# A one-core decoder step in which 14 of the weight loads are sent as transfers of 63, 63 and 2 partitions

## The reference, cut to what matters

```python
def retrieve(hb):
    q = (hb @ wq).reshape(chunk, PEER_HEADS, 2, PEER_HALF)      # 1024 -> 2048 columns
    s = jnp.einsum('nhcd,hckd->nhck', q, sk)                    # 8 heads x 2 x 128 keys
    sv, si = lax.top_k(s, 16)
    ...                                                        # the best 16 of 16x16 sums
    expert = i1 * N_KEYS + i2                                   # one of 16384 experts
    g = jax.nn.softmax(cs, axis=-1)
    act = gelu(einsum('nd,nhkd->nhk', hb, u_tab[expert]))
    return einsum('nhk,nhkd->nd', g * act, v_tab[expert])
```

## Time and profile before

| | us |
|---|---|
| median of 3 runs (lowest, highest) | 3008.63 (3007.17, 3009.83) |
| profiled execution, its own time | 3011.34 |
| its span, from the first to the last instruction | 3009.4 |
| TensorE busy in the span | 2609.7 |
| VectorE busy | 2108.1 |
| bytes moved | 1214.93 MB, mean 404 GB/s |

### The profile page before, as it was taken

The page is one execution under the profiler, slowest core; times in us unless marked ns, Lnnn a source line. Parts: engine busy times, 40 slices in busy tenths (PEclk is TensorE's granted clock), DMA queues, the critical chain, the costliest instruction groups (busy, mean ns, idle before and its releaser), DMA issues.

```text
span 3009.4 us, 27506 instructions
## 1 busy us (share of the span) xinstructions
PE 2609.7 (87%) x7369; PEld 1282.4 (43%) x7369; DVE 2108.1 (70%) x5150; ACT 1285.6 (43%) x3706; POOL 1206.2 (40%) x1104
## 2 busy tenths in 40 slices
PE   8989999999988888888899889887899977777777
PEld 6675565555544443333444434333444422222222
DVE  3546766788766667777667677778676766777666
ACT  2123444655444434444443444345443444444444
POOL 2103443444444444444443444444343434334442
PEclk9999999999999999999999999999999999999999
DMA  9979999999999999999999999999999999999997
GB/s 346 334 280 366 382 421 410 417 395 411 422 421 421 421 421 413 421 422 394 422 421 419 381 421 416 421 422 412 421 416 419 410 421 406 420 422 410 420 414 319
DMA packets 175000, 1214.93 MB, mean 404 GB/s; under 512 B 19730, under 2 KB 20766, under 8 KB 33269
## 3 DMA queue, kind: packets, MB, share of 16 engines
q0 software_dynamic: 155904, 1124.11, 91.0%
q1 hardware_dynamic: 18941, 89.07, 7.6%
HBM read 1208.47 MB, written 38.37 MB: 414 GB/s over the span
## 4 chain that ended last, share of the span: by engine, by line
DMA 45%; PE 37%; DVE 8%; ACT 6%; issue 3%; POOL 1%; another core or an unknown queue 0%; DVEq 0%; SPq 0%; ACTq 0%; POOLq 0%
DMA RING<-in_peer_uv,idx 44%; PE PSUM L1291 22%; PE PSUM L974 10%; DVE RING L1998 5%; ACT diag L1489 2%; PE PSUM L985 1%; ACT L1480 1%; ACT gate L1485 1%; PE PSUM L956 1%; ACT act_h L1480 1%; PE PSUM L1279 1%; POOL RING L922 1%; ACT L1468 1%; DMA RING<-in_peer_uv,pidx 1%; PE PSUM L995 0%
## 5 line engine op out<-in xcount | busy, mean ns | idle before, releaser
L1291 PE MATMUL PSUM<-RING,diag 128*128 128x512 f32 (+1 forms) x4096 | 1977.2, 619 | 364.4 <-ACT diag L1489 358.0
L922 POOL DMA_INDIRECT RING<-in_peer_uv,idx x1024 | 1155.8, 1129 | 1593.5 <-PE PSUM L1291 1481.2
L1998 DVE CUSTOM_DVE_ANT_0 RING<-RING,H 128x1024 f32<-128x1024 f32 x1032 | 1263.5, 1225 | 650.2 <-DMA RING<-in_peer_uv,idx 636.1
L1291 PEld LDWEIGHTS PSUM<-RING,diag 128*128 128x128 f32 (+1 forms) x4096 | 737.9, 192 | 1446.0 <-ACT diag L1489 820.3
L1480 ACT ACTIVATE act_h<-dots 128x1 f32<-128x1 f32 x1040 | 208.2, 200 | 1112.5 <-DVE dots L1998 1110.8
L1489 ACT ACTIVATE diag<-ident,gate 128x128 f32<-128x128 f32 x1008 | 404.8, 402 | 33.1 <-PE PSUM L1291 0.3
L974 PE MATMUL PSUM<-HT,WCH 128*128 128x256 f32 (+2 forms) x1408 | 335.0, 385 | 1.5 <-ACT HT L1344 1.3
L1485 ACT ACTIVATE gate<-act_h,ex 128x1 f32<-128x1 f32 x1008 | 296.8, 294 | 32.7
L974 PEld LDWEIGHTS PSUM<-HT,WCH 128*128 128x128 f32 x1408 | 265.3, 192 | 90.9 <-issue 59.2
L1480 ACT ACT_TABLE_LOAD x91 | 116.8, 1283 | 6.9 <-DVE dots L1998 5.3
L1344 ACT ACTIVATE YT<-PSUM 128x256 f32<-128x256 f32 (+4 forms) x70 | 27.4, 391 | 191.4 <-PE PSUM L974 166.8
(11 more groups left out here) (265 smaller groups left out, 1523.8 us busy)
## 6 DMA issues: line engine op xcount, KB each, us to landing
WCH<-in_peer_wq SPq DMA_DIRECT2D x28, 1024.0 KB
WCH<-in_w_in_ab SPq DMA_DIRECT2D x18, 1024.0 KB
RING<-in_peer_uv,idx POOLq DMA_INDIRECT x1024
out_win_k_sample<-in_state_win_k POOLq DMA_DIRECT2D x8, 2016.0 KB, 12.6
out_win_v_sample<-in_state_win_v POOLq DMA_DIRECT2D x8, 2016.0 KB, 12.0
RING<-in_w_in_ab SPq DMA_DIRECT2D x6, 1024.0 KB, 14.4
WCH<-in_w_out_ab SPq DMA_DIRECT2D x6, 1024.0 KB
X<-in_x_prompt SPq DMA_DIRECT2D x4, 512.0 KB, 9.4
```

Of the source, the lines that this page charges most:

```text
L922: pool.indirect_dma_start(rows[:, use % SLOTS, :], None, peer_uv.rearrange("l e n -> (l e) n"), bass.IndirectOffsetOnAxis(ap=at, axis=0),) ...
L1291: last = nc.tensor.matmul(PSUM[0:out_n, accumulator(n) + half, :], diag[:, at % DIAGS, 0:out_n], rows[:, use % SLOTS, D + half * 512:D + h ...
L1998: V.tensor_tensor_reduce(out=u, in0=u, in1=row, scale=1.0, scalar=0.0, op0=ALU.mult, op1=ALU.add, accum_out=dots[:, tau % SETS, k:k + 1]). ...
```

## The change

Two functions are new. `beside_gathers(n)` is true for the pairs 24 to 63. `load_parts(n)` gives the partition ranges in which pair n is sent: one of 128, or, where the pair is beside gathers and n divides by three, 0 to 62, 63 to 125, and 126 and 127. The three transfers go out one behind the other on the same queue, and each adds 16 to the same semaphore, so the counts that TensorE waits for are summed over the parts. The bytes, the buffers and the order are as before.

```diff
+BESIDE_GATHERS = [(kind, 1) for kind in ("p", "v", "wo")] + [("q", 1)]
+
+def load_parts(n):
+    if beside_gathers(n) and n % 3 == 0:
+        return (0, 63), (63, 126), (126, P)
+    return (0, P),
+
+def beside_gathers(n):
+    piece = chunk_list()[2 * n]
+    return piece[0:2] in BESIDE_GATHERS or piece[0:3] == ("q", 0, 1)
...
+        PARTS = [load_parts(n) for n in range(len(HOMES))]
+        def loads_by(n):
+            return sum(len(PARTS[m]) for m in range(n + 1) if HOMES[m][0] == HOMES[n][0])
...
-            eng.wait_ge(w_loaded[home], 16 * (use + 1))
+            eng.wait_ge(w_loaded[home], 16 * loads_by(CHUNKS.index(piece) // 2))
...
-            eng.wait_ge(w_loaded[home], 16 * (use + 1) if home < NW_FIRST + 3 else 32)
+            eng.wait_ge(w_loaded[home], 16 * loads_by(n) if home < NW_FIRST + 3 else 32)
...
-                    sp.dma_start(pair_buffer(home), src).then_inc(w_loaded[home], 16)
+                    for lo, hi in PARTS[n]:
+                        sp.dma_start(pair_buffer(home)[lo:hi, :, :, :], src[lo:hi, :, :, :]).then_inc(w_loaded[home], 16)
```

## The result

The change takes 3100.36 us (median of 4 runs, 3097.46 to 3101.57) against 3007.9 us for the kernel before (4 runs beside them, 3002.81 to 3009.83): ratio 1.0309, 95% interval 1.0291 to 1.0327. That is 92.5 us more, 6.6 us for each of the 14 changed loads. The forecast was 3090, the range 3028 to 3140. The profiled execution has a span of 3099.2 us, 89.8 more than before; the mean granted TensorE clock is 0.964.

What follows compares the result with a forecast made beforehand. The DMA engines, at a ceiling of 421 GB/s, were taken as the bound. Per load 1.87 us imbalance and 4.19 slow rate, 14 x 6.06 = 84.8, less 4 absorbed: 3008.6 + 81 = 3090 us, range 3028 to 3140.

Steps and rivals of the forecast that it cites:

- The ceiling: DMA beside gathers: 421 GB/s is the limit, so a microsecond of DMA work added on an engine is one of the kernel.
- Issues and counts at 0: SyncE's queue: 28 more issues, 22 us at most, are hidden by its waiting, and higher semaphore counts cost nothing; 0.
- Nine engines: Changed loads: each 63-partition transfer goes on nine engines, 14 rows each, 15 on two, none on seven.
- Imbalance, 1.87 us a load: Changed loads: the busiest engines get 6 rows more than before at 0.311 us a row, 1.87 us a load.
- The slow rate, 4.19 us a load: While a changed load runs, oddly dealt writes into SBUF slow all engines to 0.675 of the rate; 4.19 us a load.
- Less 4 us absorbed: At 589 to 626 us, where compute holds the gathers back and DMA idles, late gathers cost nothing; 4 us allowed.
- What is late next: Pair 39's load, the shortest notice at 13.8 us: TensorE may stand still 1 to 3 us; cost to the path 0.
- The signs: Line 736 and behind changed loads: 28 issues more, about 284 GB/s at share 1.0, then share falling; VectorE's wait up 80 us.
- Imbalance alone: Rival for the changed loads: nine engines but no slow rate, 22 to 27 us, 3031 to 3036 us; chance 0.17.
- The even spread: Rival for the changed loads: rows over all 16 engines, or another nine each time, 0 to 4.4 us, 3009 to 3013; chance 0.10.
- the faster case: Rival: one late engine sets the pace and is relieved of 8 rows a load, up to 35 us less, 2974; chance 0.04.
- The worse cases: Rival: fewer engines or a slower rate; seven engines 3124 us, half rate on nine 3153; beyond 3140 chance 0.09.

Runs made afterwards that it cites:

- gapless copy: Against the kernel before: whole loads, each of the 14 followed by an HBM to HBM copy of 54 rows without gaps; 3021.3 us against 3007.6.
- 40 changed loads: Against the changed kernel: all 40 pairs loaded beside gathers cut as 63, 63 and 2, not every third; 3273.37 us against 3004.24 for the kernel before.
- three column parts: Against the changed kernel: the 14 loads cut along columns into three transfers of all 128 partitions; 3008.1 us against 3007.6 for the kernel before.
- 8 x 16: Against the changed kernel: the 14 loads go as eight transfers of 16 partitions; 3115.18 us against 3007.6 for the kernel before.
- 4 x 32: Against the changed kernel: the 14 loads go as four transfers of 32 partitions; 3060.43 us against 3004.24 for the kernel before.
- 64 and 64: Against the changed kernel: the 14 loads go as two transfers of 64 partitions; 3060.67 us against 3007.6 for the kernel before.
- 126 and 2: Against the changed kernel: the 14 loads go as transfers of 126 and 2 partitions; 3043.13 us against 3004.24 for the kernel before.
- 127 and 1: Against the changed kernel: only pairs 45 and 60 cut, as 127 and 1 partitions, all others whole; 3084.86 us against 3005.31 for the kernel before.
- balanced cuts: Against the changed kernel: the 14 loads cut by partition with 8 rows an engine (64 and 64, 4 x 32, 8 x 16); 3060.67, 3060.43 and 3115.18 us.
- copy on nine engines: Against the kernel before: whole loads, each of the 14 followed by an HBM to HBM copy of nine gapped groups of 6 rows; 3026.62 us against 3004.24.

## Why the prediction was right, and where it was off

*The ceiling.* Right. Work added on the DMA engines came out in the time: 13.7 of 14.7 us with the gapless copy, and 6.6 and 6.7 us a load with 14 and 40 changed loads.

*Issues and counts at 0.* Right: three column parts cost 0.0 (interval 0.999 to 1.001).

*Nine engines.* Right. In every kernel the packets of q1 fit one completing packet for each engine used: the change has 4 more a load, 9 + 9 + 2 - 16. 8 x 16 gives 112 more (8 x 16 - 16), 4 x 32 gives 48, 64 and 64 gives 16, 126 and 2 none (14 + 2), 127 and 1 gives 14 fewer. This count and the 39.8 us of the 127-partition load are what the traces show of it; no view used here has a row for each engine. By the rule cited ahead (the Trainium skill, "DMA: Bandwidth & Descriptors", section "Why a DMA increments its semaphore by 16 and not by 1": the largest number up to 16 that divides the slowest dimension) 63 gives 9, 126 gives 14 and 127 gives 1, and the runs agree in all three.

*Imbalance, 1.87 us a load.* There, but smaller. The page of the change has 14 us of idle time, 16 to 19 against the -2 to -5 of the balanced cuts: 1.1 to 1.4 a load, and the kernel with 40 changed loads gives about the same (43 us). The copy on nine engines came to 1.6 a load with its own bytes in it.

*The slow rate, 4.19 us a load.* Mechanism right, the rate right in the mean, size too small. Here is the slow stretch of pair 48's load as one:

```profile
1124.00:1137.50 13.50, 9.19 (x24) 4.57 (x24) 3.73 (x10) 2.12 (x7) 2.93 (x4) 0.87 1.01 282
```

282/421 = 0.67, and over the 14 us that begin 3.5 us behind the issue all 14 changed loads lie between 269 and 292 GB/s, 0.666 of 421 in the mean. So "I take 0.675, from the nearest row" held for the whole load, though the 301 and 243 inside it show that the row hit a mean and not a constant; and 64 and 64 or 8 x 16, at 235 and 204, show that it isn't the rate of every such transfer. The term that was mis-sized is the time for which it holds, and with it the 4.19: the slow stretch lasts some 14 us and not 12.90, 14 x (1 - 0.666) = 4.7 us, and the page's packet time grew by 76 us, 5.4 a load. What makes it longer stays open.

*Less 4 us absorbed.* Not to be seen: 40 loads cost 6.7 each, no less than 14 did. The idle time that I read at 589 to 626 us was not used up either. It belongs to the same step of the work, which now comes some 24 us later, and there it stands again: the DMA share is 0.67 in the worst 10 us, where it was 0.74.

```profile
640.00:650.00 10.00, 10.00 (x29) 5.67 (x29) 2.21 (x6) 3.90 (x13) 4.67 (x4) 0.88 0.67 227
```

So the forecast's 81 us lay near the 92.5 partly by luck. Against the page, the slow packets were put 17 us too low and the absorbed time took off 4 that weren't absorbed, but the imbalance was put 7 to 10 us too high (26 us for 16 to 19), which hid a third to a half of that.

*What is late next.* Right in place and in the length of the wait; its cost is open. I had TensorE wait 1 to 3 us at pair 39 at no cost to the path. The first fence is the chain of waits in the changed kernel, the second the timeline of weight loads into TensorE, with the idle time before it in brackets.

```profile
792.17 17.68 DMA WCH<-in_w_out_ab
```

```profile
809.89 1.59 PEld L1006 LDWEIGHTS PSUM<-WCH,YT 128*128 128x128 f32 x8 [2.06 <-DMA WCH<-in_w_out_ab]
```

The load lands 17.7 us behind its last issue (I had 13 to 16) and TensorE's weight load stands for 2.06 us. Before, the chain of waits ran through TensorE's accumulations there, from 734 to 792 us; now it runs through this load, so the trace does not show the wait to be free. What speaks for little or nothing is that the DMA share stays at 1.00 to 1.02 from 805 to 825 us. It was not tried by itself.

*The signs.* 28 issues more, rate near 284 at share 1.0, full rate between loads, VectorE's wait up by about the loss, 6.6 us a load where 4 to 9 were given: all there. One was misplaced: I put the fall of the share at the end of the 13 us. It comes at 1143 to 1148, 22 us and more behind the issue, after a stretch at 422. I take it that the seven relieved engines first work through the gathers in their queues and only then have none. For it speaks that the dearer but balanced 8 x 16 has no such fall: its share is 0.99 to 1.01 over the 20 us behind its slow stretch.

*The rivals.* Imbalance alone (3031 to 3036) came out in its nearest experiment as 3026.62, 22.4 us over the kernel before; it is a quarter at most of the change. The even spread and the faster case are out by the packet count and by the time. The worse cases, with seven engines or half the rate, didn't come either: nine engines by the count, 0.67 by the rate.

**What the slow rate is.** Cuts with the same bytes and an even or nearly even load of the engines cost 0.0, 2.8, 3.8, 4.0 or 7.7 us by which partitions go in one transfer. So it is neither the issues (three by columns cost nothing), nor the number of transfers up to four (2 and 4 cost the same), nor the balance, nor DMA traffic as such (424 GB/s beside the copy). For eight transfers one row an engine is a rival that wasn't tried by itself; against it, 32 completing packets more a load, from two transfers to four, cost 0.2 us, and from four to eight there are 64 more for 3.7 us; the cut by columns has 288 packets more a load in q1 (22973 against 18941 in all) and costs nothing. What is left, by elimination, is how rows and engines are paired: where in SBUF each engine writes, or which rows of HBM it reads, and these two were not separated. One mechanism of the first kind fits the order: the gathers give each engine a fixed set of partitions, and a load dealt otherwise makes an engine write where another's gathers go.

The Trainium skill, "SBUF — State Buffer", section "Door 1: The DMA port swizzle", has 16 ports for DMA, each serving two groups of four partitions that lie 32 apart, with bit 6 choosing the other port of a pair. By it a block of 64 or of 32 partitions reaches eight ports, a block of 16 only four, and 126 all of them. So 16 engines write through eight, eight and four ports, and 14 engines through 16: the order measured (3.8, 4.0, 7.7; 2.8). For the change it gives about as many writers as ports, nine and eight, and yet packet time grew by 5.4 us a load: the count of writers to a port ranks the balanced cuts, but doesn't give the change's price. No row shows a port, so the mechanism is the one that fits and not one that was seen.

Open: why all 16 engines slow down alike (share 1.0 at 235 GB/s) and not only those that meet; why the upper 63 partitions cost more than the lower (the idle engines' own gathers going there would do it, but this wasn't separated). Not tried: cutting the 96-partition loads of the opening, each of which has one of 32 partitions beside it that I hadn't read into the earlier trace rows, or the 120-partition load of the pooling state otherwise; these are the places where the kernel before itself may pay this price. No version faster than the kernel before was found.

## What to carry to other kernels

Where gathers to 128 partitions keep the DMA engines full, load SBUF in 128-partition transfers and cut, if at all, along the free dimension: that was free, while the cuts by partition cost 2.8 to 7.7 us per MB, even in powers of two, and 127 and 1 cost 39.8. Look at share and rate together behind a suspect transfer: rate down at share 1.0 is slow packets, rate and share down together is idle engines. A count with a poor divisor (63, and far worse 127) adds imbalance to it. A price read from one odd transfer is good for the shape it was read from, and a sum that comes out near the time can still have its terms wrong both ways.

## What the runs showed of the hardware that I had not expected

- Halves of 64 partitions, as regular as a cut can be, run at 235 GB/s beside gathers, slower than the 289 of 126 partitions on 14 engines.
- In the kernel with 127 and 1, two issues on SyncE's queue took 40 and 41 us where 0.33 is usual. Both are those of the one-partition part, right behind the 127 (at 946.64 and 2250.36 us). So a large transfer on one engine seems to hold up the queue that issues it (count: shortest/median/longest ns, from and to us):

```profile
L757 SPq DMA_DIRECT2D WCH<-in_peer_wq x30: 250/328/41177, 173.5 to 2403.7; - x30
```

- By the packets, a copy from HBM to HBM without gaps was spread over 16 engines though its outermost dimension was nine; with gaps it stayed on nine (32 and 18 packets a copy).
